# Moving the split modulated input h by 16 and 8 bytes in SBUF, layer by layer

## The reference

```python
# layers 0 and 1
h = rmsnorm(x, norm1_g[l]) * (1.0 + sc1) + sh1
x = x + g1 * token_mix(h, w_in[l], w_fourier[l], w_ret[l], w_out[l])
h = rmsnorm(x, norm2_g[l]) * (1.0 + sc2) + sh2
x = x + g2 * conv_ffn(h, ffn_up[l], conv_w[l], conv_b[l], ffn_down[l])
# layers 2 and 3 (256 tokens, in layer 2 also 256 context tokens)
p, u, vs, q, k, v, gl = jnp.split(modulate(rms_norm(h, norm1_g[l]), sh1, sc1) @ w_in[l], SPLIT_POINTS, axis=-1)
h = h + g1 * mix          # pooling, gating unit and neighbourhood attention, merged, @ w_o
h = h + g2 * sq_relu_mlp(modulate(rms_norm(h, norm2_g[l]), sh2, sc2), w_ff1[l], w_ff2[l])
```

## Time and profile before

| | |
|---|---|
| median of 3 runs | 2086.85 us (2086.14 to 2087.07) |
| span of the profiled execution | 2087.3 us |
| TensorE matmul busy | 2056.7 us, 14232 records |
| TensorE weight load busy | 1892.2 us |
| VectorE busy | 1509.2 us |
| ScalarE busy | 986.2 us |
| GpSimd busy | 390.6 us |
| granted TensorE clock, mean | 0.995 of full speed |
| HBM read | 393.08 MB, 189 GB/s over the span |

### The profile page before, as it was taken

The page is one execution under the profiler, slowest core; times in us unless marked ns, Lnnn a source line. Parts: engine busy times, 40 slices in busy tenths (PEclk is TensorE's granted clock), DMA queues, the critical chain, the costliest instruction groups (busy, mean ns, idle before and its releaser), DMA issues.

```text
span 2087.3 us, 36942 instructions
## 1 busy us (share of the span) xinstructions
PE 2056.7 (99%) x14232; PEld 1892.2 (91%) x14232; DVE 1509.2 (72%) x2169; ACT 986.2 (47%) x1500; POOL 390.6 (19%) x284
## 2 busy tenths in 40 slices
PE   8999999999999999999999999999999999999998
PEld 8999999999999999999877888988888998899998
DVE  7777889977767999978988524898533376866554
ACT  4544456635445465553245533442233245756453
POOL 0421203300601213324101002130020021122020
PEclk9999999999999999999999999999999999999999
DMA  9775767776566656663554322366532254664552
GB/s 334 290 254 192 260 223 245 254 280 220 205 233 220 204 201 213 202 225 133 188 172 142 111 86 93 122 200 224 191 111 95 68 182 157 212 217 162 188 186 102
DMA packets 109739, 396.36 MB, mean 190 GB/s; under 512 B 12425, under 2 KB 13073, under 8 KB 109329
## 3 DMA queue, kind: packets, MB, share of 16 engines
q1 hardware_dynamic: 108304, 389.99, 55.3%
q0 software_dynamic: 1280, 4.20, 0.6%
HBM read 393.08 MB, written 1.05 MB: 189 GB/s over the span
## 4 chain that ended last, share of the span: by engine, by line
PE 83%; DVE 12%; DMA 2%; ACT 1%; issue 1%; POOL 0%; SPq 0%; DVEq 0%; ACTq 0%; POOLq 0%
PE bank L492 21%; PE bank L493 21%; PE bank L494 21%; DVE w_lo L1430 5%; PE bank L591 2%; PE bank L592 2%; PE bank L593 2%; DVE stage L1451 2%; PE bank L653 1%; PE bank L656 1%; DMA stage<-in_stream 1%; DVE rstd L1448 1%; PE bank L516 1%; PE bank L515 1%; PE bank L513 1%
## 5 line engine op out<-in xcount | busy, mean ns | idle before, releaser
L1430 DVE TENSOR_TENSOR w_lo<-stage,w_hi 128x1024 fp32r<-128x1024 f32 x536 | 710.1, 1339 | 433.6 <-ACT w_hi L999 432.7
L999 ACT ACTIVATE w_hi<-stage 128x1024 fp32r<-128x1024 f32 x536 | 565.6, 1059 | 863.6 <-PE bank L494 575.3
L492 PE MATMUL bank<-h_hi,w_hi 128*128 128x256 f32 (+1 forms) x2560 | 782.5, 306 | 11.1 <-DVE w_lo L1430 6.3
L494 PE MATMUL bank<-h_hi,w_lo 128*128 128x256 f32 (+1 forms) x2560 | 777.0, 304 | 0.0
L493 PE MATMUL bank<-h_lo,w_hi 128*128 128x256 f32 (+1 forms) x2560 | 776.9, 303 | 0.0
L492 PEld LDWEIGHTS bank<-h_hi,w_hi 128*128 128x128 f32 x2560 | 483.5, 189 | 41.2 <-DVE w_lo L1430 9.8
L494 PEld LDWEIGHTS bank<-h_hi,w_lo 128*128 128x128 f32 x2560 | 484.0, 189 | 21.6
L493 PEld LDWEIGHTS bank<-h_lo,w_hi 128*128 128x128 f32 x2560 | 483.1, 189 | 21.7 <-issue 0.5
L1451 DVE SCALAR_TENSOR_TENSOR stage<-stage,cvec 128x1024 f32<-128x1024 f32 x192 | 259.7, 1355 | 11.3 <-DMA cols<-in_cols 8.3
L492 PE MATMUL bank<-f_hi,w_hi 128*128 128x256 f32 (+1 forms) x448 | 146.6, 327 | 0.0
L493 PE MATMUL bank<-f_lo,w_hi 128*128 128x256 f32 (+1 forms) x448 | 146.6, 327 | 0.0
(11 more groups left out here) (248 smaller groups left out, 3239.3 us busy)
## 6 DMA issues: line engine op xcount, KB each, us to landing
stage<-in_stream SPq DMA_DIRECT2D x728, 512.0 KB, 4.3
bias<-in_bias POOLq DMA_DIRECT2D x16, 256.0 KB, 3.1
cvec<-in_cvec SPq DMA_DIRECT2D x3, 512.0 KB, 4.3
X<-in_x SPq DMA_DIRECT2D x2, 512.0 KB, 5.7
decay<-in_decay SPq DMA_DIRECT2D x1, 1024.0 KB, 5.4
X<-in_x SPq DMA_DIRECT2D x1, 1024.0 KB, 7.8
out<-X SPq DMA_DIRECT2D x4, 256.0 KB, 2.1
rope<-in_rope SPq DMA_DIRECT2D x2, 256.0 KB, 4.8
```

The costliest lines, as they stand in the source:

```text
L492: mm(out, w_hi[:, slot, w], xh[:, c, 0:T], start=first, stop=False)
L494: last = mm(out, w_lo[:, slot, w], xh[:, c, 0:T], start=False, stop=final)
L999: A(w_hi[:, m % NR, :], stage[:, n % NS, :], ACT.Copy).then_inc(hi_ready, 1)
L1430: do(V.tensor_tensor(w_lo[:, m % NR, :], stage[:, n % NS, :], w_hi[:, m % NR, :].bitcast(F32), ALU.subtract), unit_done, done_value(n))
```

## The change

The two tiles of h are placed through a helper that allocates a flat tile at a 32-byte address and views it a few words (`h_skip`) further in. No instruction is added, removed or moved on any engine; operands' addresses are all that differs.

```diff
-        h_at = [edge + off for off in (448, 448, 512, 448)]
+        h_at = [edge + off for off in (448, 416, 512, 448)]
+        h_skip = (4, 4, 0, 2)
         assert where[0] <= min(h_at)
-        h_hi = operands("h_hi", [P, DC, T2], h_at)
-        h_lo = operands("h_lo", [P, DC, T2], [at + HBYTES for at in h_at])
-        where[0] = max(h_at) + 2 * HBYTES
+
+        def inside(name, at):
+            flat = [sb(f"{name}_{n}", [P, skip + DC * T2], F32R, a) for n, (a, skip) in enumerate(zip(at, h_skip))]
+            return [f[:, skip:skip + DC * T2].rearrange("p (c t) -> p c t", c=DC) for f, skip in zip(flat, h_skip)]
+
+        h_hi = inside("h_hi", h_at)
+        h_lo = inside("h_lo", [at + HBYTES for at in h_at])
+        where[0] = max(h_at) + 2 * HBYTES + 32
```

## The result

| | before | after |
|---|---|---|
| median of 4 runs | 2086.49 us | 2104.44 us |
| range | 2077.11 to 2087.07 us | 2102.77 to 2105.27 us |
| profiled span | 2087.3 us | 2102.6 us |

The ratio is 1.011, with a 95% interval of 1.0085 to 1.0134. The forecast was 2073 us, so faster. One run of the kernel before took 2077 us, 9 us less than the three known ahead of the prediction. That spread turned out to be part of the answer.

A forecast was written before the change was run, and what follows sets the result against it. TensorE's step from one matmul's start to the next was taken to bound the kernel. The profiled span of 2087.3 us less 10.6 (h) and 3 (tiles above h) gave 2073.7 us, 2073 for the median; range 2050 to 2104 us.

The forecast's parts named there:

- What bounds the kernel: TensorE, busy 99% of the span; what counts is the step between matmul starts, 113.3 to 120.6 ns for 256 columns.
- What one h matmul will cost: h matmuls of 256 columns, layers 0, 1, 3: steps of 115.0 or 114.2 ns, 12.1 us less, net 10.6 us.
- the larger end piece is paid: Extra cycles equal the larger piece a 128-byte boundary cuts from the moving row's ends: 32 at offset 0, 16 at 64.
- a lock between the regular rhythms of the two reading streams, which an odd piece breaks: Reading of the long 117.7 ns step at offset 64; breaking it saves 10.7 us in layers 0 and 1, 3.5 in 3.
- What lies above h: u, r, b and f move by 32 bytes: 24 cycles extra at offsets 96 and 32, entered as 3 us less.
- the extra does not grow with the columns: Step time beyond the columns at 2.4 GHz is paid once per matmul: about 32 cycles at offset 0, 16 or 26 at 64.
- What was costed at nothing: Loads of h in token_block, 3 us either way for 10 cycles; ScalarE and VectorE writes of h, below 1 us.
- The counts of long and short matmuls: Of 6528 h matmuls in layers 0, 1, 3, 4963 take the long step (117.7 ns), 1565 the short (113.3 ns).
- about 1.5 us is lost again: Part of layer 1's gain returns as TensorE waits for w_lo, since VectorE is busy 145.8 of 150 us there.
- rival 1: The long step stays and the pieces cost as forecast: 119.5 ns for those h matmuls, 2095 us; chance 0.14.
- rival 2: An unaligned row costs a further piece, 6.6 ns on each of 6528 to 10000 matmuls: 2130 to 2150 us; chance 0.11.
- Rival 3: Nothing changes, as stalls alone choose the rhythm and a few words don't matter: 2087 us; chance 0.15.

The follow-up runs named there:

- b1: Kernel before with both weight tiles 64 bytes higher; h moved 128 bytes up, so keeping its offset; u, r, b, f unmoved: 2111.82 us, ratio 1.0168.

## Why the prediction was wrong, point by point

**What bounds the kernel** was right: steps of TensorE in layers without waits, read from counts in stretches. Both kernels differ by steps, and waits moved the other way.

**"What one h matmul will cost" failed.** The value taken, 115.0 ns at offsets 48 and 80 and 114.2 ns at 72, came from two points (offsets 0 and 64) and a rule laid through them, that the larger end piece is paid. Measured are means of 119.1, 119.2 and 120.5 ns (29.8, 30.2 and 33.3 cycles on 106.7 ns). The term was -10.6 us and is +19 us by steps. Of the half-sentence "a lock between the regular rhythms of the two reading streams, which an odd piece breaks" one half came out: the 26.7 cycles are gone and the 192 ns weight load is 189. But the 16 cycles are gone as well, and what took the place of both is steady stretches of 30 cycles in layers 0 and 1 and of 32 and 36 in layer 3, where the rule had 20 and 18. And the rule named the wrong quantity, the row's place; b1 shows that it is the distance to the loaded row. The sign of being wrong that was set for it, layers 0 and 1 answering with opposite signs, did not come (+4.3 and +7.1 us): both moves by 16 bytes did the same, as the rule had it, but the other way.

**"What lies above h" failed in sign.** The forecast was -3 us, measured is +7.8 us by steps, and 0.29% alone. The largest piece is 768 matmuls of 512 columns in layer 2, for which the forecast had 24 cycles at offset 32 and which pay 48. That the 32 bytes move these tiles at all was read from the diff, and was right. The 256-column rows of layer 2 did gain, 5.7 cycles as against 8. Here a premise of the whole working fails, "the extra does not grow with the columns": it holds at offset 0, where it was read, with 32 cycles for 256 and for 512 columns. At offset 32 it is 26 and 48.

**What was costed at nothing** held for the writers of h (510 and 479 ns), and about for the loads from h in `token_block`: with steps of up to 80 cycles counted, the extra of the 512-column matmuls rose from 38.2 to 44.7 cycles in layer 0, from 37.7 to 39.9 in layer 1 and from 37.6 to 41.7 in layer 3. That is 0.5 us and twice 0.2 us on 192, 192 and 96 matmuls, within the 3 us given.

**The counts of long and short matmuls**, from mean durations, were 4963 and 1565; by starts 1689 were short. That is near enough for this trace, but the kernel before has no such count: it was 2321 and 3094 in its other traces. What the prediction left out is that the kernel before itself has a spread of 16 us (2072.6 to 2088.6 us in 29 runs on one chip), as large as the 14 us that it forecast. A slip without effect: the price of offset 0, 120.0 ns, does not lie between the 120.6 and 120.4 ns named beside it; by starts it is 120.0 (32.0 cycles).

**The waits** were meant for a gain ("about 1.5 us is lost again") and worked on the loss instead: some 10 of 26.7 us came back.

**Rivals.** The measured 2104 us lie just outside the stated range, between rival 1 (2095, 119.5 ns for what was long) and rival 2 (2130). Rival 1's price for the h matmuls, 119.5 ns, is near the 119.1 to 120.5 measured, but by another mechanism. Rival 3 and the rule named beside it fall: the Trainium skill, "SBUF — State Buffer", specifications, counts lines of 16 bytes, and layers 0 and 1 moved by whole lines and lost 4.3 and 7.1 us.

**Open.** Why the extras have the values 16, 21.3, 24, 25.2, 26.7, 28, 30, 32, 36 and 48 and what unit of memory lies behind them is not settled. That distances of 64 modulo 128 are special is shown for weights at 0 and at 64 only. By 256, all distances of 64 that had the short rhythm have remainder 192, the offsets 32 to 112 of the table stand for 160 to 240, and only offset 0 for 0; b1 hints that this matters, and no run was made for it.

## What to carry to other kernels

Where TensorE streams split operands without a pause, the place of a moving tile relative to the loaded one was worth 1 to 2% of this kernel, and a move by 4 bytes counted; measure each offset that is meant to be used, and don't lay a rule through two of them. When a tile is moved, list the addresses of all others behind it: here a slack of 32 bytes that nobody needed cost 0.3%. If two stretches of one program at one address have different steps, take several traces of the kernel before ahead of any comparison: here the three traces chose differently.

## What was not expected of the hardware

- One program had 512 and 532 matmuls in the same 60 us of layer 0 in two executions, with the granted clock at 1.00 in both: 117.7 and 113.3 ns a step. Its steady stretches had one of these two steps and none between.
- A single matmul of 128 columns, 0.06 us long, changed the step of the 96 of its block by 4.4 ns each, in either direction, block after block in the feed-forward part of layer 0.
- A move of 4 bytes (offset 64 to 68) raised the mean extra of 2400 matmuls to 32.1 cycles; weights moved by 64 bytes against h made the patterns of layer 0 and layer 2 change places, at 1.7% of the time.
